# Transposes one weight piece later, and one split ahead of its convolution, in the up stage of an FFN

## What is computed

```python
def depthwise_conv_centred(h, w, b):          # CONV_WIDTH = 3, along the 256 tokens
    out = b
    for t in range(CONV_WIDTH):
        out = out + hp[:, t:t + S] * w[t]
    return out

def conv_gated_ffn(h, w_up, conv_w, conv_b, w_down):
    a = depthwise_conv_centred(h @ w_up, conv_w, conv_b)   # h 256 x 2048, w_up 2048 x 11264
    g, u = jnp.split(a, 2, axis=-1)
    return (jax.nn.silu(g) * u) @ w_down
...
mod = (jax.nn.silu(c) @ w_ada[i] + b_ada[i])       # of the second block, 2048 x 12288, two rows
```

## Time and profile before

| | before |
|---|---|
| median of 3 runs | 4007.4 us |
| span of the profiled execution | 4009.0 us |
| TensorE (PE) busy | 3717.9 us, 93% |
| VectorE (DVE) busy | 2477.5 us, 62% |
| ScalarE (ACT) busy | 1747.8 us, 44% |
| GpSimd (POOL) busy | 646.0 us, 16% |
| mean granted TensorE clock | 0.948 |

### The profile page before, as it was taken

The page is one execution under the profiler, slowest core; times in us unless marked ns, Lnnn a source line. Parts: engine busy times, 40 slices in busy tenths (PEclk is TensorE's granted clock), DMA queues, the critical chain, the costliest instruction groups (busy, mean ns, idle before and its releaser), DMA issues.

```text
span 4009.0 us, 44645 instructions
## 1 busy us (share of the span) xinstructions
PE 3717.9 (93%) x16234; PEld 2965.1 (74%) x16234; DVE 2477.5 (62%) x2262; ACT 1747.8 (44%) x1927; POOL 646.0 (16%) x379
## 2 busy tenths in 40 slices
PE   6989999998998989999998998999988889999998
PEld 5867777776777867777776777787753678888886
DVE  3655888988444654888888545236665555555454
ACT  4444565555433444655555433224421334333333
POOL 0001445453000001554444000000000000000000
PEclk9989999998999989999998999979988999999999
DMA  5535667665554534676666554235500345656564
GB/s 193 168 109 172 226 228 245 221 229 184 178 187 158 168 115 163 228 239 224 226 224 205 164 186 137 82 105 179 194 0 0 134 139 180 187 180 186 180 186 147
DMA packets 349116, 687.26 MB, mean 171 GB/s; under 512 B 15935, under 2 KB 20048, under 8 KB 347728
## 3 DMA queue, kind: packets, MB, share of 16 engines
q1 hardware_dynamic: 301136, 593.50, 44.7%
q10 hardware_dynamic: 47872, 92.29, 6.9%
HBM read 683.64 MB, written 2.10 MB: 171 GB/s over the span
## 4 chain that ended last, share of the span: by engine, by line
issue 47%; PE 24%; DVE 11%; DVEq 7%; POOLq 5%; DMA 3%; ACT 2%; ACTq 1%; POOL 1%; SPq 0%
POOLq L588 5%; DVE ada_sum L1105 4%; DVEq L1318 4%; PE acc L1994 3%; PE acc L1995 3%; PE acc L1996 3%; PE acc L1778 3%; PE acc L1780 3%; PE acc L1779 3%; DMA ada_raw<-in_w_ada 2%; DVE w_lo L1048 2%; DVEq L1295 2%; PE acc L2231 1%; PE side L2241 1%; DVE conv L1294 1%
## 5 line engine op out<-in xcount | busy, mean ns | idle before, releaser
L1048 DVE TENSOR_TENSOR w_lo<-w_raw,w_hi 128x2048 fp32r<-128x2048 f32 x362 | 816.2, 2258 | 568.1 <-ACT w_hi L621 567.5
L621 ACT ACTIVATE w_hi<-w_raw 128x2048 fp32r<-128x2048 f32 x362 | 678.6, 1879 | 569.8 <-DMA w_raw<-in_w_down 273.6
L1778 PE MATMUL acc<-w_hi,in_h 128*128 128x512 f32 x2112 | 866.0, 410 | 15.2 <-DVE in_l L1057 12.9
L1779 PE MATMUL acc<-w_lo,in_h 128*128 128x512 f32 x2112 | 855.2, 405 | 0.0
L1780 PE MATMUL acc<-w_hi,in_l 128*128 128x512 f32 x2112 | 854.0, 404 | 0.0
L587 POOL TENSOR_TENSOR ada_sum<-ada_sum,ada_term 128x512 f32<-128x512 f32 x330 | 553.4, 1677 | 393.0 <-ACT ada_term L793 351.7
L1105 DVE SCALAR_TENSOR_TENSOR ada_sum<-ada_raw,silu_c,ada_sum 128x512 f32<-128x512 f32 x330 | 487.6, 1478 | 36.0 <-issue 11.0
L1778 PEld LDWEIGHTS acc<-w_hi,in_h 128*128 128x128 f32 x2112 | 410.6, 194 | 116.2 <-issue 14.4
L1780 PEld LDWEIGHTS acc<-w_hi,in_l 128*128 128x128 f32 x2112 | 409.3, 194 | 101.2
L1779 PEld LDWEIGHTS acc<-w_lo,in_h 128*128 128x128 f32 x2112 | 410.6, 194 | 97.3
L1741 DVE TENSOR_TENSOR w_lo<-w_raw,w_hi 128x2048 fp32r<-128x2048 f32 x126 | 288.4, 2291 | 293.2 <-ACT w_hi L1024 293.2
(11 more groups left out here) (303 smaller groups left out, 4141.8 us busy)
## 6 DMA issues: line engine op xcount, KB each, us to landing
w_raw<-in_w_up SPq DMA_DIRECT2D x176, 1024.0 KB, 5.1
w_raw<-in_w_mlp SPq DMA_DIRECT2D x128, 1024.0 KB, 5.3
w_raw<-in_w_in SPq DMA_DIRECT2D x100, 1024.0 KB, 5.1
ada_raw<-in_w_ada ACTq DMA_DIRECT2D x176, 512.0 KB, 4.4
w_raw<-in_w_down SPq DMA_DIRECT2D x64, 1024.0 KB, 5.1
w_raw<-in_w_o SPq DMA_DIRECT2D x32, 1024.0 KB, 5.1
w_raw<-in_w_down SPq DMA_DIRECT2D x32, 768.0 KB, 4.5
w_raw<-in_w_out SPq DMA_DIRECT2D x16, 1024.0 KB, 5.1
```

The costliest lines, as they stand in the source:

```text
L621: nc.scalar.activation(hi[s][:, 0:n], raw[s][:, 0:n], ACT.Copy).then_inc(w_hi[s], 1)
L1048: nc.vector.tensor_tensor(lo[s][:, 0:n], raw[s][:, 0:n], hi[s][:, 0:n].bitcast(F32), ALU.subtract).then_inc(w_lo[s], 1)
L1778: nc.tensor.matmul(acc[p][i][:], ah_[:, kt, tok], hi[s][:, k], start=(kt == 0), stop=False)
L1779: nc.tensor.matmul(acc[p][i][:], ah_[:, kt, tok], lo[s][:, k], start=False, stop=False)
```

## The change

On ScalarE and VectorE, `split_up(3)` now comes ahead of the convolution of the pair before (`centre(before, 1)`, `finish_pair(before)`), and `split_up(7)` ahead of that of chunk 0 (`centre(j, 0)`, `outer_taps(j, 0)`). On TensorE, the transposes of chunk 1 of the pair before, with `ada_total`, come after the second piece of chunk 0 and not after the first, and the transposes of chunk 0 after the second piece of chunk 1. No instruction is added or removed; the loads issued by ScalarE and SyncE keep their order.

```diff
@@ ScalarE, up_pair
                 split_up(2)
+                split_up(3)
                 if before is not None:
                     centre(before, 1)
-                split_up(3)
                 ctx_terms(0)
...
                 ctx_terms(3)
+                split_up(7)
                 centre(j, 0)
-                split_up(7)
                 load_ada(5)
@@ TensorE, up_pair
                 for s in range(NS):
                     product(0, s, r, in_h, in_l, 4 * s, 4, KT)
-                    if s == 0 and before is not None:
+                    if s == 1 and before is not None:
                         turn_chunk(before, 1)
                         ada_total(l * NPAIR + before)
...
                 for s in range(NS):
                     product(1, s, r + 1, in_h, in_l, 4 * s, 4, KT)
-                    if s == 0:
+                    if s == 1:
                         turn_chunk(j, 0)
```

## The result

The changed kernel takes 4036.68 us (median of 4 runs, 4034.98 to 4039.14). Against runs of the kernel before on the same chip the ratio is 1.0076, interval [1.006, 1.0092]: slower by 30 us (24 to 37). The prediction was 4034. The profiled execution spans 4033.0 us where that of before spanned 4009.0, so +24 us between the two traces.

A forecast was written before the change was run, and what follows sets the result against it. VectorE was taken to bound the up stage. Loop pairs of 55.23 + 0.6 + 0.3 = 56.1 us add 10.3 and 8.2 us, first pairs 7.8: together +26 us on the median 4007.4, 4034 us; range 3998 to 4046.

The forecast's parts named there:

- ten long and ten short ones: Loop pairs before: long ones wait 0.51 us before split 6; short ones lack it, last four sums taking 5.72 us.
- What bounds the stage: Up stage: VectorE is full and sets the pace; TensorE's 44.7 us of waits for `y` are worth nothing.
- The rival by which TensorE sets the pace: Up stage: waits of 44.7 us and half-clock time go, 79 us gained, 3928 us; chance 0.14 together with the faster rival.
- The loop of ada 7 and split 2: Pair start: ada 7, ScalarE's split 2, VectorE's split 2 close a loop; its 2.65 us wait is untouched by the change.
- TensorE late next at split 2: After the moved transposes TensorE waits for `w_lo` instead, at no path cost; VectorE's 0.51 us before split 6 goes.
- The SiLU chain: Taps of chunk 0, SiLU, ScalarE's split 8: no longer covered by split 7, +0.6 us a pair, bounds 0 and +0.9.
- Split 3 ahead of the finish: Pair start: split 4 runs into GpSimd's second sum, +0.3 us a pair, bounds -0.5 and +0.7.
- The last four ada sums: Pair end: the last load lands quickly with TensorE early, so 6.60 us in every pair; other bound 5.72.
- The first pair: First pair of each layer: later chunk-0 transposes delay taps, SiLU's table load and split 8, +3.9 us, bounds +0.6 and +5.
- Cancelling: Rival, loop pairs: every pair becomes like the short one, gains and losses cancel, 4009 us; chance 0.22.
- Fewer contended sums: Rival, ada sums: two more escape GpSimd, 1.7 us a pair, 3999 or 3981 us; chance 0.14 with the TensorE-pace rival.
- Late transposes as a price of 1 us times 20: Rival, ScalarE's `centre`: transposes late beyond 2 us of slack, each us costing 20 us, 4050 us and more; chance 0.06.

The follow-up runs named there:

- split7_only: Kernel before with only split 7 moved ahead of the centre and taps of chunk 0, on ScalarE and VectorE; 4024.19 us, ratio 1.0041.
- after_silu_behind: Changed kernel with ScalarE's split 8 ahead of SiLU; 3997.04 us, ratio 0.9973 against the kernel before.
- split3_only: Kernel before with only split 3 moved ahead of the finish of the pair before, on ScalarE and VectorE; 4012.2 us, ratio 1.0007.
- chunk1_only: Kernel before with only the transposes of chunk 1 a piece later; 3993.83 us, ratio 0.9971.
- before_early_split2: Kernel before with ScalarE's split 2 ahead of load_ada(1), the load that waits for ada 7; 3971.69 us, ratio 0.9917.
- best: Kernel before with later chunk-1 transposes, split 7 ahead of chunk 0's taps, SiLU behind ScalarE's split 8, split 2 ahead of load_ada(1); 3941.18 us, ratio 0.9848.
- tensor_part: Kernel before with only both sets of transposes one piece later, splits unmoved; 4019.56 us, ratio 1.0025.
- chunk1_early: Kernel before with chunk-1 transposes a piece later and ScalarE's split 2 ahead of load_ada(1); 3990.18 us, ratio 0.9964.
- two_products: Changed kernel with TensorE leaving out the hi x lo product in the up stage, a third of its matmuls there; 4020.82 us, ratio 1.0042 against the kernel before.

## Why the prediction was right

The forecast of 4034 us was met because its terms were met: with the means of the table the loop pairs cost 10.5 and 8.3 us, forecast 10.3 and 8.2, and the first pairs cost 3.9 us (layer 0) and 4.4 us, forecast 3.9 each. Two of the terms came out by luck in part, as their reasons did not hold: split 3 and the last four sums, below. The picture of the kernel before was also too simple. Its pairs do not fall into ten long and ten short ones: of 18 traced, six wait for more than 0.35 us before split 6 (0.51 to 1.34), and in five others the last load is late and the wait before split 2 is 3.6 us. In layer 0 these are two of the nine waits that the prediction counted as 2.65. The sum was not hurt, since it used the measured mean pair of before.

**What bounds the stage: right.** It said that VectorE is full and TensorE's wait is worth nothing. Taking the wait away alone gave +10 us, with 5 us lost in each first pair and nothing won in the others; a third less matmul work made the pair 0.1 us shorter. The rival by which TensorE sets the pace (3928 us) is out. The Trainium skill, "TensorE: Matmul & The Clock Gate", section "Why this matters for your kernels", advises against idle gaps because the clock falls. The trace agrees with it on the clock (0.93 to 0.95 in the stage, 1.97 to 1.03 us for the transposes, and 0.50 behind the new gap of 2.92 us), and the time went up all the same, since the engine that it speeds was not the one waited for.

**The loop of ada 7 and split 2: right.** It was said to be untouched, and stands at 2.65 us in every pair; opening it took 33 us from the kernel before and 54 from the changed one.

**TensorE late next at split 2: right.** The new waits are for `w_lo`, 2.92 us before piece 2. The wait of VectorE before split 6 went, and the alternation with it: pairs of 56.14 us, all alike.

**The SiLU chain, +0.6 us a pair: right.** From the start of the taps or of split 7 to split 8 it was 8.39 us and is 8.93, so +0.54. Over 1 us of idle time before split 8 was forecast, 1.23 was measured. Alone the move gave +16 us, half of the loss (split7_only), and with SiLU behind split 8 the loss was gone and turned to a gain (after_silu_behind).

**Split 3 ahead of the finish, +0.3 us: the size about right, by luck, the step wrong.** The prediction had split 4 run into GpSimd's second sum, 2.5 us or more. Split 4 takes 2.28 us. What it missed is GpSimd's first sum: begun 0.04 us after ada 0's first operation, it no longer meets a split but that operation, 1.36 us for 0.98. That is +0.38 us. It had put the lower bound there, expecting this operation to get shorter. Alone, split 3 made no difference clear of noise (split3_only, +3 us). The estimate that the prediction drew from the Trainium skill, "SBUF — State Buffer", section "Who interferes with whom", about +0.6 us, had GpSimd's second sum wait and then go ahead of split 4. That case did not arise, so the rule is neither borne out nor refuted here: GpSimd's second sum (441.90 to 443.19) ends before split 4 begins at 443.66.

**The last four ada sums, 6.60 us in every pair: the number right (6.63), the condition for it wrong.** The prediction said that the load lands quickly when the refill of a slot was issued some 5 us before it, and that an early TensorE brings this about. The first half is what the traces show. The last piece load and the last conditioning load ahead of these sums are issued 1.4 us apart in the short pair of before:

```profile
579.43 0.37 SPq L439 DMA_DIRECT2D w_raw<-in_w_up  x1
```

```profile
580.80 0.38 ACTq L786 DMA_DIRECT2D ada_raw<-in_w_ada  x1
```

and 5.1 us apart in the changed kernel:

```profile
470.16 0.37 SPq L439 DMA_DIRECT2D w_raw<-in_w_up  x1
```

```profile
475.28 0.38 ACTq L786 DMA_DIRECT2D ada_raw<-in_w_ada  x1
```

In layer 0 of before, after, split7_only, chunk1_only, before_early_split2 and best, the four sums take 6.5 us or more wherever the two issues are 2.7 us or more apart, and 4.9 to 6.0 us wherever they are 0.5 to 1.4 us apart. At 2.15 us (tensor_part) both occur, and one pair each of split3_only and chunk1_early does not fit. This is read from traces and was not tried by itself. The second half fails: in tensor_part and chunk1_only TensorE is early and the load is late all the same in most pairs, and in before_early_split2 TensorE is late in five of nine pairs and no load is. What counts is where the two issues fall, and the prediction had no row that fixed this for the changed kernel.

**The first pair, +3.9 us: right.** 3.9 us in layer 0 and 4.4 in layer 1, from TensorE's transposes of chunk 0 through the table load to split 8, with the forecast 2 us before the taps (1.98). In two_products, with less work for TensorE, t1 comes 4.3 us earlier.

**The rivals.** Cancelling is what chunk1_only shows, and it falls as soon as split 7 moves too. Fewer contended sums did occur, but in ada 4 alone: two sums of 1.59 us with split 7 at 2.28 in every pair, 0.77 us a pair, which the gap before split 8 took up (after_silu_behind); the other sums take 3.3 us for two as before. Late transposes as a price of 1 us times 20 were not seen in the changed kernel, but of 1.4 to 2.0 us they are what struck chunk1_early.

## What to carry to other kernels

A wait of the engine with the highest busy share can be worth nothing, as here, when another engine walks through the same stretch without a gap: read that engine's timeline for one period before you value the wait, and let each kernel's period, times the number of periods, account for the total. In an engine that runs in order, look at what stands between a wait and the work that others need: a small operation (SiLU) or a load whose buffer is not yet free, ahead of a split on the path, made a wait of 1.23 and 2.65 us a pair here, and each went by exchanging two lines. An order is good only together with the others: the later transposes gained 12 us alone, lost 19 beside the early split 2, and are part of the fastest kernel, where split 7 came in time (what they are worth there was not tried by itself).

## What the runs showed of the hardware

In this kernel operations of VectorE and of GpSimd on SBUF are longer where they overlap, and which of the two pays depends on how they lie. GpSimd's first sum took 2.85 us beneath a split and 1.04 us beneath a sum of rows, which itself went from 0.98 to 1.36 us. Moving split 3 by one place thus shifted a cost to another instruction. Moving split 7 took one away: it takes 2.28 us and the two sums behind it 1.59, where it had been 2.98 and 1.59, or 2.28 and 2.36. And TensorE's mean granted clock went from 0.95 to 0.86 in the stage where a third of its matmuls was left out, so that its busy time per matmul rose from 470.88 / 2060 = 0.229 to 375.57 / 1472 = 0.255 us: an engine that waits for others can run at a lower clock without making the time longer (mean pair 56.01 us against 56.12).
